# w_out's last halves and the first query group, one token tile after the other, in the layers of the second block

## The chip, the core and the metric

The program runs on one core of a Trainium2 chip. The metric is the device time in microseconds (us) of one execution. PE is TensorE, DVE is VectorE, ACT is ScalarE, POOL is GpSimd, and SP is SyncE, which only issues transfers here.

## The reference

x is 256 tokens of 1024 features. A first block (attention mixer and convolutional FFN) is followed by two layers of a second block; the change lies in these layers.

```python
def rms_norm_2(x, g):
    xf = x.astype(jnp.float32)
    y = xf * lax.rsqrt(jnp.mean(xf * xf, axis=-1, keepdims=True) + EPS)
    return (y * g.astype(jnp.float32)).astype(x.dtype)
...
    merged = gates[:, :, 0] * (oa @ w_branch_na) + gates[:, :, 1] * (ob @ w_branch_swa)
    return merged @ w_out
...
        q = (xc @ w_query).reshape(PEER_CHUNK, PEER_HEADS, 2, half)
        s = jnp.einsum('thpk,pnk->thpn', q, sub_keys).astype(jnp.float32)
        sv, si = lax.top_k(s, PEER_TOPK)
...
        top_s, sel = lax.top_k(cand, PEER_TOPK)
        eidx = jnp.take_along_axis(cidx, sel, axis=-1)
        g = jax.nn.softmax(top_s, axis=-1)
        u = expert_down[eidx]
        vv = expert_up[eidx]
        act = jax.nn.gelu(jnp.einsum('td,thkd->thk', xc, u).astype(jnp.float32), approximate=False)
        return jnp.einsum('thk,thkd->td', (g * act).astype(x.dtype), vv)
...
        x = x + token_mixer(rms_norm_2(x, norm_mix[l]), ...)
        x = x + peer_ffn(rms_norm_2(x, norm_ffn[l]), ...)
```

Each token has 8 heads, and for each head 16 experts are picked out of 16384 by two lists of 128 keys. An expert has a down and an up row of 1024 numbers each. The next layer starts from x when all experts of this one are added.

## The kernel before

**Tiles and exactness.** The 256 tokens are two tiles of 128. Each product with a weight is done in three passes (`product`): weights and features are split into a high part, rounded by ACT (`split_hi`, L517), and a low part, the difference, made by DVE (`split_lo`, L530). `w_lo` counts low parts, `half_done` counts halves that PE has used up.

**Weights.** All weights form one stream of halves of 512 KB, two for a group of 256 output columns. Three slots `W` hold raw halves, `WH` and `WL` hold their parts. Within a layer, halves 42 to 49 are w_out, and 50 to 65 are the query projection, of eight groups. In w_out the order is `WO_ORDER`: groups 0 and 1 take their halves in turn (42 to 45), then group 2 (46, 47) and group 3 (48, 49). SP issues the loads in stream order; half n can be loaded into its slot when the low part of half n-3 is made. Nine query halves (57 to 65) are loaded ahead into places of their own, `HELD`: held half e is issued just behind the load of half 44+e. The last, e = 8, lies over the gains of the norm, so SP first waits until DVE has used those of all column groups (L1059, as `n_peer.hn`). Halves 53 to 56 stand behind it in SP's order.

**End of the mixer.** `wo_pe` (L905) does each half for both tiles. After a group DVE adds the result to `x` (L1965) and multiplies by the gain into `h_norm` (L1972; the norm's factor is applied later). PE turns two chunks of `h_norm` with four transposes (`turned_pe`, L895), ACT copies them as high part (L1609), DVE makes the low part (L1954). Of the first query group PE takes chunks as they become ready, with the weights as the stationary operand (`first_part`), then scores tile 0 against both lists of keys (L1282).

**From scores to gathers.** DVE finds the 8 best of each list (L2069, L2070). The sum of the two best is the first expert: its row goes to POOL at once (L2113), the other seven of the first eight after some 15 more small instructions (L2103). POOL gathers 128 rows of 8 KB with one indirect transfer (L1098) into one of eight ring slots, 512 times in all: 16 for each head and tile. A slot comes free when DVE has made its dot product (L2143, L2166), ACT has made a diagonal matrix of the weight, and PE has added its up rows (L1315). Each later gather into a slot waits for this. ACT's squares of `x` (L1649), whose sum gives the norm, wrote into `Y`, where slots 4 and 5 of the ring lie; the other seven rows therefore waited for them.

The order on every engine is the order in which the code issues, as written by hand.

## Time and profile before

| | us |
|---|---|
| median of 3 runs | 2240.69 (2240.04 to 2241.07) |
| profiled execution, its own time | 2241.91 |
| its span | 2240.1 |
| PE busy | 1990.3 (89%) |
| DVE busy | 1609.4 (72%) |
| ACT busy | 1144.5 (51%) |
| POOL busy | 874.5 (39%) |
| gathers' queue, share of 16 DMA engines' span | 57.8% (536.90 MB) |
| SP's and ACT's queue | 22.4% (157.63 MB) |

Busy shares are means over stages with different limits. The gathers run from 734.6 to 2232 us with a break between the layers. Below, times are from the span's start.

### The profile page before, as it was taken

How to read it: one execution, taken by the hardware profiler on the slowest of the kernel's cores; microseconds unless marked ns; L12 is line 12 of the kernel's file. 1: busy time of each engine (PE TensorE's matmuls, PEld its weight loads, DVE VectorE, ACT ScalarE, POOL GpSimd, SP SyncE). 2: the span in 40 equal slices, each digit the busy share in tenths (PEclk: the TensorE clock that was granted, in tenths of full speed). 3: DMA queues.
4: the chain of work that ended last, by engine and by line, in shares of the span. 5: the costliest groups of instructions: out<-in, count | busy, mean ns of one | idle time of the engine just before them, and what ended most of it. 6: DMA issues, size and time to landing. Idle time of an engine off the chain costs nothing.

```text
span 2240.1 us, 29611 instructions
## 1 busy us (share of the span) xinstructions
PE 1990.3 (89%) x9760; PEld 1302.1 (58%) x9798; DVE 1609.4 (72%) x3230; ACT 1144.5 (51%) x2534; POOL 874.5 (39%) x557
## 2 busy tenths in 40 slices
PE   9999999999999898977777788999899887778877
PEld 8999899998889644422222223889644432222222
DVE  4566777777787877776777765787887776777774
ACT  4455555545554655454454545565655444444443
POOL 0120000000230355566667663040355566666664
PEclk9999999999999999999999999999999999999999
DMA  7544465665636999999999997736899999999998
GB/s 247 172 132 142 148 184 180 185 189 157 219 119 219 381 421 421 421 421 421 421 418 422 420 421 302 233 116 222 334 421 421 421 421 421 422 422 411 422 421 338
DMA packets 120772, 707.23 MB, mean 316 GB/s; under 512 B 13664, under 2 KB 13920, under 8 KB 55008
## 3 DMA queue, kind: packets, MB, share of 16 engines
q0 software_dynamic: 73728, 536.90, 57.8%
q1 hardware_dynamic: 43488, 157.63, 22.4%
q10 hardware_dynamic: 3456, 11.40, 1.5%
q8 instruction: 57, 0.93, 0.2%
q14 instruction: 43, 0.35, 0.0%
HBM read 704.84 MB, written 1.05 MB: 315 GB/s over the span
## 4 chain that ended last, share of the span: by engine, by line
PE 41%; DMA 25%; POOL 11%; DVE 9%; issue 8%; ACT 6%; POOLq 0%; SPq 0%; DVEq 0%; ACTq 0%
DMA work<-in_experts,expert_idx 24%; PE ps L548 11%; POOL work L1098 10%; PE ps L549 10%; PE ps L550 10%; PE ps L1315 6%; DVE work L2166 2%; DVE weights_lo L533 2%; PE ps L687 1%; ACT L1616 1%; ACT L1667 1%; DMA weights<-in_wstream 1%; ACT arena L1672 1%; DVE work L2143 1%; PE ps L713 1%
## 5 line engine op out<-in xcount | busy, mean ns | idle before, releaser
L1315 PE MATMUL ps<-work,arena 128*128 128x512 f32 x2040 | 989.9, 617 | 216.1 <-ACT arena L1672 212.4
L1098 POOL DMA_INDIRECT work<-in_experts,expert_idx x512 | 790.2, 1543 | 621.2 <-PE ps L1315 291.3
L1315 PEld LDWEIGHTS ps<-work,arena 128*128 128x128 f32 x2040 | 359.0, 191 | 821.0 <-ACT arena L1672 516.2
L2166 DVE CUSTOM_DVE_ANT_0 work<-h_norm,work 128x1024 f32<-128x1024 f32 x480 | 588.1, 1225 | 334.5 <-DMA work<-in_experts,expert_idx 320.2
L1667 ACT ACTIVATE small<-small 128x1 f32<-128x1 f32 x512 | 150.2, 293 | 609.1 <-DVE small L2166 588.0
L533 DVE TENSOR_TENSOR weights_lo<-weights,weights_hi 128x1024 fp32r<-128x1024 f32 x280 | 349.8, 1255 | 152.8 <-ACT weights_hi L528 152.1
L548 PE MATMUL ps<-feat_hi,weights_hi 128*128 128x256 f32 x1528 | 445.3, 291 | 7.6 <-DVE weights_lo L533 5.8
L528 ACT ACTIVATE weights_hi<-weights 128x1024 fp32r<-128x1024 f32 x280 | 295.0, 1056 | 286.0 <-PE ps L550 232.6
L549 PE MATMUL ps<-feat_lo,weights_hi 128*128 128x256 f32 x1528 | 432.8, 283 | 0.0
L550 PE MATMUL ps<-feat_hi,weights_lo 128*128 128x256 f32 x1528 | 432.7, 283 | 0.0
L548 PEld LDWEIGHTS ps<-feat_hi,weights_hi 128*128 128x128 f32 x1528 | 293.3, 192 | 18.1 <-issue 9.3
L549 PEld LDWEIGHTS ps<-feat_lo,weights_hi 128*128 128x128 f32 x1528 | 293.6, 192 | 5.4 <-issue 4.8
L550 PEld LDWEIGHTS ps<-feat_hi,weights_lo 128*128 128x128 f32 x1528 | 293.5, 192 | 0.0
L1087 POOL TENSOR_TENSOR work<-arena,consts 128x640 f32<-128x640 f32 x8 | 13.9, 1769 | 525.3 <-issue 445.8
L1672 ACT ACTIVATE arena<-consts,small 128x128 f32<-128x128 f32 x512 | 205.5, 401 | 16.7
L1669 ACT ACTIVATE small<-small,expert_gate 128x1 f32<-128x1 f32 x512 | 150.7, 294 | 16.7
L754 POOL TENSOR_TENSOR work<-work,small 128x1024 f32<-128x1024 f32 (+2 forms) x26 | 60.0, 2310 | 197.3 <-DVE small L744 197.3
L548 PE MATMUL ps<-weights_hi,feat_hi 128*128 128x256 f32 (+2 forms) x416 | 131.4, 316 | 1.8 <-DVE feat_lo L465 0.9
L549 PE MATMUL ps<-weights_lo,feat_hi 128*128 128x256 f32 (+2 forms) x416 | 128.2, 308 | 0.0
L550 PE MATMUL ps<-weights_hi,feat_lo 128*128 128x256 f32 (+2 forms) x416 | 128.2, 308 | 0.0
L1786 DVE SCALAR_TENSOR_TENSOR work<-ps,params,work 128x254 f32<-128x254 f32 (+1 forms) x128 | 55.8, 477 | 51.8 <-ACT work L1469 47.6
L548 PEld LDWEIGHTS ps<-weights_hi,feat_hi 128*128 128x128 f32 x416 | 79.6, 191 | 7.1 <-DVE weights_lo L533 1.5
(250 smaller groups left out, 1912.1 us busy)
## 6 DMA issues: line engine op xcount, KB each, us to landing
weights<-in_wstream SPq DMA_DIRECT2D x280, 512.0 KB, 4.2
work<-in_experts,expert_idx POOLq DMA_INDIRECT x512
arena<-in_wstream SPq DMA_DIRECT2D x12, 512.0 KB, 6.0
arena<-in_na_bias ACTq DMA_DIRECT2D x6, 512.0 KB, 5.3
params<-in_wstream SPq DMA_DIRECT2D x6, 512.0 KB, 5.9
arena<-in_bias ACTq DMA_DIRECT2D x5, 512.0 KB, 4.6
params<-in_par ACTq DMA_DIRECT2D x2, 576.0 KB, 5.3
params<-in_par ACTq DMA_DIRECT2D x1, 1024.0 KB, 6.7
```

Source lines behind the costliest of these rows:

```text
L528: nc.scalar.activation(WH[:, n % SLOTS, :], raw(n), ACT.Copy).then_inc(w_hi, 1)
L533: nc.vector.tensor_tensor(WL[:, n % SLOTS, :], raw(n), WH[:, n % SLOTS, :], ALU.subtract).then_inc(w_lo, 1)
L548: nc.tensor.matmul(out, stat[0], mov[0], start=start, stop=False)
L549: nc.tensor.matmul(out, stat[0], mov[1], start=False, stop=False)
L550: return nc.tensor.matmul(out, stat[1], mov[0], start=False, stop=stop)
L754: nc.gpsimd.tensor_tensor(part, part, view(rsum[b.turn][:, r0:r1], [1, r1 - r0], [0, b.width]), ALU.mult).then_inc(A.probs, 1)
L1098: nc.gpsimd.indirect_dma_start(ring[:, r, :], None, experts, bass.IndirectOffsetOnAxis(ap=EIDX[:, b, c * RING + r:c * RING + r + 1], axis= ...
L1315: ins = nc.tensor.matmul(bank(2 * t + h), DIAG[:, r, :], ring[:, r, D + h * 512:D + (h + 1) * 512], start=False, stop=False)
L1667: nc.scalar.activation(ga[:, r:r + 1], hd[:, r:r + 1], ACT.Gelu, scale=rstd[:, t:t + 1]).then_inc(gelu_ready, 1)
L1669: nc.scalar.activation(gw8[:, r:r + 1], ga[:, r:r + 1], ACT.Copy, scale=GWT[:, b, c * RING + r:c * RING + r + 1]).then_inc(w_ready, 1)
L1672: nc.scalar.activation(DIAG[:, r, :], ident, ACT.Copy, scale=gw8[:, r:r + 1]).then_inc(diag_ready, 1)
L2166: nc.vector.tensor_tensor_reduce(ring[:, r, 0:D], HN[:, t, :], ring[:, r, 0:D], 1.0, 0.0, ALU.mult, ALU.add, hd[:, r:r + 1]).then_inc(dots ...
```

## The change

w_out's halves 46 to 49 are first used for tile 0 alone, then for tile 1; only half 46 for tile 1 stands between them. The first query group is done tile by tile, with the features as stationary operand (its weights are packed so), for tile 0 after half 46's second use, and for tile 1 after all of w_out. Its result then has tokens on the partitions, so PE turns it back (`query0_turned`) between two copies by ACT. Because halves 46 to 48 stay in use longer, their parts lie in room that the ring of gathers takes later (`SPARE`), so the splits of 49 to 51 wait for a half six places back, not three. The adds to `x` and the gains are split by tile for groups 2 and 3. `h_norm` is now counted in six turns, and SP's wait before held half 8 is for the sixth, group 3 of tile 1. The squares go to `arena` and the wait for them is moved behind the index of the seven rows. Held 7 still waits for groups 0 and 1. Tile 1's keys of the first head move behind query group 1.

```diff
+        with nc.sbuf_tensor("work_rounded", [P, 16392], F32R) as work_rounded:
+            SPARE = [work_rounded[:, a:a + 2 * HW] for a in (0, 8200, 14344)]
...
+        def spare(n):
+            local = (n - L_HALF) % L_HALVES - 2 * LG_WO - 4
+            return local if n >= L_HALF and 0 <= local < SLOTS else None
+        def behind_spare(n):
+            return n >= L_HALF and SLOTS <= (n - L_HALF) % L_HALVES - 2 * LG_WO - 4 < 2 * SLOTS
+        def high(n):
+            return WH[:, n % SLOTS, :] if spare(n) is None else SPARE[spare(n)][:, 0:HW]
+        def low(n):
+            return WL[:, n % SLOTS, :] if spare(n) is None else SPARE[spare(n)][:, HW:2 * HW]
...
-            if n >= SLOTS:
-                act.wait_ge(half_done, base + n - SLOTS + 1)
-            nc.scalar.activation(WH[:, n % SLOTS, :], raw(n), ACT.Copy).then_inc(w_hi, 1)
+            if n >= SLOTS and spare(n) is None:
+                act.wait_ge(half_done, base + n - (2 * SLOTS if behind_spare(n) else SLOTS) + 1)
+            nc.scalar.activation(high(n), raw(n), ACT.Copy).then_inc(w_hi, 1)
...
+        HN_TURNS, HI_TURNS = WO + 2, 7
+        def hn_turn(g, t=TT - 1):
+            return (1, 2, 3 + 2 * t, 4 + 2 * t)[g]
+        def turned_pe(pe, nm, l, g, tiles=range(TT)):
+            pe.wait_ge(nm.hn, HN_TURNS * l + hn_turn(g, tiles[0]))
             for c in (2 * g, 2 * g + 1):
-                for t in range(TT):
+                for t in tiles:
                     ins = nc.tensor.transpose(ps[:, c * S + t * P:c * S + (t + 1) * P], HN[:, t, c * P:(c + 1) * P], ident)
...
+        def wo_tile(pe, n, t, b, at, chunks=range(HC)):
+            h = WO_ORDER[n][1]
+            w = split_pe(pe, L_HALF + 2 * LG_WO + n, at)
+            for i in chunks:
+                c = h * HC + i
+                ins = product(ps[:, b * 512 + t * GC:b * 512 + (t + 1) * GC], kept(c, t * P, P), cols(w, i * GC, GC), c == 0, c == KC - 1)
+            return ins
...
-                        sp.wait_ge(n_peer.hn, 4 * l + -(-min(gains_end, D) // GC))
+                        sp.wait_ge(n_peer.hn, HN_TURNS * l + hn_turn(-(-min(gains_end, D) // GC) - 1))
...
-                wo_pe(pe, (lproj_taken, l * N2 + L_PROJ + L_GATE), G_LAYER + LG_WO, l, at, turned=n_peer)
+                taken0 = WO + (WO + 1) * l
+                for n in range(4):
+                    wo_both(pe, (lproj_taken, l * N2 + L_PROJ + L_GATE), G_LAYER + LG_WO, n, l * BR + BR, at)
+                pe.wait_ge(wo_taken, taken0 + 1)
+                wo_tile(pe, 4, 0, 6, at)
+                turned_pe(pe, n_peer, l, 0)
+                wo_tile(pe, 5, 0, 6, at).then_inc(tile0_done, 1)
+                turned_pe(pe, n_peer, l, 1)
+                wo_tile(pe, 6, 0, 5, at).then_inc(tile0_done, 1)
+                turned_pe(pe, n_peer, l, 2, (0,))
+                wo_tile(pe, 7, 0, 5, at).then_inc(tile0_done, 1)
+                wo_tile(pe, 4, 1, 6, at).then_inc(half_done, 1)
+                turned_pe(pe, n_peer, l, 3, (0,))
...
+                def query0(t, b):
+                    for c in range(KC):
+                        if c % HC == 0:
+                            w = split_pe(pe, L_HALF + 2 * LG_PQ + c // HC, at)
+                        if c % 2 == 0:
+                            pe.wait_ge(n_peer.hT, HI_TURNS * l + (1 if c == 0 else c // 2 + 1 + 3 * t))
+                        ins = product(ps[:, b * 512:b * 512 + GC], feat(c, t * P, P), cols(w, c % HC * GC, GC), c == 0, c == KC - 1)
+                        if t and c % HC == HC - 1:
+                            ins.then_inc(half_done, 1)
                     return ins
+                def query0_turned(t, step):
+                    pe.wait_ge(first_query, step)
+                    for part in range(2):
+                        ins = nc.tensor.transpose(ps[:, 5 * 512 + S + part * P:5 * 512 + S + (part + 1) * P], pqT[:, 4 + t, part * P:(part + 1) * P], ident)
+                    ins.then_inc(tile0_done, 1)
...
-                pe.wait_ge(n_peer.hT, l * 4 + 2)
-                parts = [split_pe(pe, L_HALF + 2 * LG_PQ, at)]
-                first_part(0, range(HC))
-                turned_pe(pe, n_peer, l, 3)
-                parts.append(split_pe(pe, L_HALF + 2 * LG_PQ + 1, at))
-                first_part(1, range(HC))
-                pe.wait_ge(n_peer.hT, l * 4 + 3)
-                for part in range(2):
-                    first_part(part, range(4, 6))
-                pe.wait_ge(n_peer.hT, l * 4 + 4)
-                for part in range(2):
-                    first_part(part, range(6, 8)).then_inc(half_done, 1)
-                pe.wait_ge(first_query, l + 1)
+                query0(0, 7).then_inc(tile0_done, 1)
+                wo_tile(pe, 5, 1, 6, at, range(2))
+                query0_turned(0, l * 3 + 1)
+                wo_tile(pe, 5, 1, 6, at, range(2, HC)).then_inc(half_done, 1)
+                pe.wait_ge(first_query, l * 3 + 2)
                 key_score(4, 0, 0, 0).then_inc(first_scored, 1)
-                pe.wait_ge(lproj_taken, l * N2 + L_PROJ + L_GATE + 1)
                 key_score(5, 0, 0, 1).then_inc(first_scored, 1)
-                for part in range(2):
-                    ins = key_score(3, part, 1, part)
-                ins.then_inc(sc_done, 1)
+                wo_tile(pe, 6, 1, 7, at).then_inc(half_done, 1)
+                wo_tile(pe, 7, 1, 7, at).then_inc(half_done, 1)
+                turned_pe(pe, n_peer, l, 2, (1,))
+                turned_pe(pe, n_peer, l, 3, (1,))
+                query0(1, 6)
+                query0_turned(1, l * 3 + 3)
...
+                turned_act(0, 1, (0, TT))
+                act.wait_ge(tile0_done, l * 6 + 2)
+                turned_act(1, 2, (0, 1))
+                act.wait_ge(tile0_done, l * 6 + 3)
+                turned_act(2, 3, (0, 1))
+                turned_act(3, 4, (0, 1))
+                query0_act(0)
+                query0_turned_act(0)
+                act.wait_ge(half_done, wo_halves + 7)
+                turned_act(1, 2, (1, TT))
+                act.wait_ge(half_done, wo_halves + 8)
+                turned_act(2, 5, (1, TT))
                 split_hi(act, L_HALF + 2 * LG_PQ + 2, at)
+                turned_act(3, 6, (1, TT))
...
+                query0_act(1)
                 hi_query(SLOTS)
+                query0_turned_act(1)
+                act.wait_ge(x_ready, l * 3 + 2 * TT + 1)
+                for t in range(TT):
+                    ins = nc.scalar.activation((DIAG.rearrange("p r n -> p (r n)") if t else SC[:, 1:5, :, :].rearrange("p a s n -> p (a s n)")), X[:, t, :], ACT.Square, accum_out=ssq[:, t:t + 1])
+                ins.then_inc(n_peer.sq, 1)
+                hi_query(SLOTS + 1)
+                act.wait_ge(n_peer.var, l + 1)
+                nc.scalar.activation(std, ssq, ACT.Sqrt).then_inc(n_peer.std, 1)
...
+                for n in range(SLOTS, SLOTS + 3):
+                    half_lo(n)
+                added(0, 6, (0, TT), (half_done, wo_halves + wo_done(0)), 1)
+                half_lo(6)
+                half_lo(7)
+                added(1, 7, (0, TT), (half_done, wo_halves + wo_done(1)), 2)
+                half_lo(8)
+                lower(0, 1, (0, TT))
+                added(2, 6, (0, 1), (tile0_done, l * 6 + 1), 3)
+                half_lo(9)
+                lower(1, 2, (0, 1))
+                added(3, 5, (0, 1), (tile0_done, l * 6 + 3), 4)
+                lower(2, 3, (0, 1))
+                lower(3, 4, (0, 1))
...
+                added(2, 6, (1, TT), (half_done, wo_halves + 6), 5)
+                added(3, 7, (1, TT), (half_done, wo_halves + 8), 6)
                 rc.link(nc.vector.tensor_tensor(cand[:, 0:HALF * HALF].rearrange("p (a b) -> p a b", a=HALF), view(sv[:, 0, :], [1, HALF], [0, HALF]),
                                                 view(sv[:, 1, :], [0, HALF], [1, HALF]), ALU.add))
                 rc.link(nc.vector.max(topv[:, 0:HALF], cand[:, 0:HALF * HALF]))
                 rc.link(nc.vector.max_index(sel[:, 0, 0:HALF], topv[:, 0:HALF], cand[:, 0:HALF * HALF]))
-                pick_rows(0, HALF, 3, 1, (n_peer.sq, l + 1)).then_inc(first_rows, 1)
+                lower(1, 5, (1, TT))
+                lower(2, 6, (1, TT))
+                pick_rows(0, HALF, 3, 1).then_inc(first_rows, 1)
+                lower(3, 7, (1, TT))
+                lo_query(2)
                 lo_query(SLOTS)
+                dve.wait_ge(n_peer.sq, l + 1)
```

DVE at the end of w_out, before. `h_norm<-x,params` is the gain of a column group; `weights_lo` is a low part.

```order
L533 TENSOR_TENSOR weights_lo<-weights,weights_hi 128x1024 [waits w_hi] x2
L1965 TENSOR_TENSOR x<-x,ps 128x2x256 [waits half_done]
L1972 TENSOR_TENSOR h_norm<-x,params 128x2x256 [waits wo_taken]
L533 TENSOR_TENSOR weights_lo<-weights,weights_hi 128x1024 [waits w_hi] x2
L1965 TENSOR_TENSOR x<-x,ps 128x2x256 [waits half_done]
L1972 TENSOR_TENSOR h_norm<-x,params 128x2x256 [waits wo_taken]
L1954 TENSOR_TENSOR feat_lo<-ps,feat_hi 128x512 [waits n_peer_hi] x2
L533 TENSOR_TENSOR weights_lo<-weights,weights_hi 128x1024 [waits w_hi]
L1965 TENSOR_TENSOR x<-x,ps 128x2x256 [waits half_done]
L1972 TENSOR_TENSOR h_norm<-x,params 128x2x256 [waits x_ready]
L1954 TENSOR_TENSOR feat_lo<-ps,feat_hi 128x512 [waits n_peer_hi] x2
L533 TENSOR_TENSOR weights_lo<-weights,weights_hi 128x1024 [waits w_hi]
```

DVE at the same place, now; `128x256` and `128x2x128` are pieces for one tile.

```order
L561 TENSOR_TENSOR weights_lo<-weights,weights_hi 128x1024 [waits w_hi]
L2061 TENSOR_TENSOR x<-x,ps 128x2x256 [waits half_done]
L2063 TENSOR_TENSOR h_norm<-x,params 128x2x256 [waits wo_taken]
L561 TENSOR_TENSOR weights_lo<-weights,weights_hi 128x1024 [waits w_hi]
L2048 TENSOR_TENSOR feat_lo<-ps,feat_hi 128x512 [waits n_peer_hi]
L2061 TENSOR_TENSOR x<-x,ps 128x256 [waits tile0_done]
L2063 TENSOR_TENSOR h_norm<-x,params 128x256 [waits wo_taken]
L561 TENSOR_TENSOR weights_lo<-weights,weights_hi 128x1024 [waits w_hi]
L2048 TENSOR_TENSOR feat_lo<-ps,feat_hi 128x2x128 [waits n_peer_hi]
L2061 TENSOR_TENSOR x<-x,ps 128x256 [waits tile0_done]
L2063 TENSOR_TENSOR h_norm<-x,params 128x256 [waits wo_taken]
L2048 TENSOR_TENSOR feat_lo<-ps,feat_hi 128x2x128 [waits n_peer_hi] x2
```

The gain of group 1, second of the first piece, now stands behind one more low part (half 49); groups 2 and 3 come first for tile 0.

ACT at the end of w_out and in the first query group, before. `feat_hi<-ps` copies turned groups; `arena<-ps 128x256` takes a query.

```order
L528 ACTIVATE weights_hi<-weights 128x1024 [waits half_done,w_landed2]
L528 ACTIVATE weights_hi<-weights 128x1024 [waits half_done,w_landed0]
L1609 ACTIVATE feat_hi<-ps 128x512 [waits n_peer_transposed,half_done]
L1609 ACTIVATE feat_hi<-ps 128x512 [waits n_peer_transposed]
L528 ACTIVATE weights_hi<-weights 128x1024 [waits half_done,w_landed1]
L1609 ACTIVATE feat_hi<-ps 128x512 [waits n_peer_transposed,half_done]
L1609 ACTIVATE feat_hi<-ps 128x512 [waits n_peer_transposed]
L528 ACTIVATE weights_hi<-weights 128x1024 [waits half_done,w_landed2]
L1639 ACTIVATE arena<-ps 128x256 [waits half_done] x2
L528 ACTIVATE weights_hi<-weights 128x1024 [waits half_done,w_landed0]
L1645 ACTIVATE arena<-ps 128x256 [waits sc_done]
```

ACT at the same place, now.

```order
L556 ACTIVATE weights_hi<-weights 128x1024 [waits half_done,w_landed2]
L556 ACTIVATE weights_hi<-weights 128x1024 [waits half_done,w_landed0]
L556 ACTIVATE weights_hi<-weights 128x1024 [waits half_done,w_landed1]
L1685 ACTIVATE feat_hi<-ps 128x512 [waits n_peer_transposed]
L1685 ACTIVATE feat_hi<-ps 128x2x128 [waits n_peer_transposed,tile0_done] x2
L1685 ACTIVATE feat_hi<-ps 128x2x128 [waits n_peer_transposed]
L1690 ACTIVATE arena<-ps 128x256 [waits tile0_done]
L1695 ACTIVATE arena<-ps 128x2x128 [waits tile0_done]
L1685 ACTIVATE feat_hi<-ps 128x2x128 [waits n_peer_transposed,half_done] x2
L556 ACTIVATE weights_hi<-weights 128x1024 [waits half_done,w_landed2]
L1685 ACTIVATE feat_hi<-ps 128x2x128 [waits n_peer_transposed]
```

The splits of halves 49, 50 and 51 now stand together ahead of the first copy of turned features; the copies of query and turned query follow, and the split of half 52 comes after w_out's last half.

## Rows read from the trace of the kernel before

**Rows 1.** Windows, layer 0: length, busy time by engine, PEclk, DMA share, GB/s.
```profile
704.00:720.80 16.80, 16.77 (x138) 16.45 (x138) 11.26 (x13) 7.17 (x8) 0.00 (x0) 1.00 0.94 346
720.80:727.00 6.20, 5.64 (x46) 5.44 (x47) 4.93 (x7) 2.63 (x4) 0.00 (x0) 1.00 0.04 15
727.00:733.40 6.40, 6.17 (x52) 5.98 (x52) 3.50 (x10) 3.64 (x6) 0.00 (x0) 1.00 0.92 321
733.40:736.00 2.60, 2.17 (x19) 1.97 (x17) 2.33 (x15) 1.74 (x2) 1.11 (x1) 1.00 0.05 22
736.00:738.75 2.75, 0.00 (x0) 0.00 (x0) 1.27 (x4) 1.39 (x4) 0.26 (x1) 1.00 0.88 265
738.75:742.50 3.75, 3.64 (x19) 3.64 (x20) 3.34 (x16) 1.15 (x2) 3.14 (x3) 0.58 0.96 321
...
785.00:800.00 15.00, 14.92 (x59) 8.48 (x58) 11.98 (x31) 8.49 (x22) 9.70 (x8) 1.00 1.01 418
```

**Rows 2.** The same windows in layer 1.
```profile
1569.60:1575.80 6.20, 5.86 (x49) 5.54 (x48) 4.83 (x7) 2.71 (x5) 0.00 (x0) 1.00 0.04 13
1575.80:1582.00 6.20, 5.97 (x51) 5.78 (x50) 3.40 (x10) 3.56 (x6) 0.00 (x0) 1.00 0.91 336
1582.00:1584.50 2.50, 2.27 (x19) 2.07 (x18) 2.23 (x14) 2.43 (x4) 0.98 (x1) 1.00 0.02 8
```

**Rows 3.** Timeline of POOL: start, length, instruction, idle time before and what ended it.
```profile
734.59 1.11 POOL L1098 DMA_INDIRECT work<-in_experts,expert_idx  x1 [68.74 <-DVE expert_idx L2113]
738.50 1.12 POOL L1098 DMA_INDIRECT work<-in_experts,expert_idx  x1 [2.79 <-DVE expert_idx L2103]
...
754.13 1.34 POOL L1098 DMA_INDIRECT work<-in_experts,expert_idx  x1 [5.03 <-PE ps L1315]
...
774.87 1.03 POOL L1098 DMA_INDIRECT work<-in_experts,expert_idx  x1 [2.38 <-DVE expert_idx L2046]
```

**Rows 4.** Timeline of DVE, from h_norm's second group to the second index.
```profile
714.51 0.69 DVE L1972 TENSOR_TENSOR h_norm<-x,params 128x512 f32<-128x512 f32 x1
715.63 1.23 DVE L533 TENSOR_TENSOR weights_lo<-weights,weights_hi 128x1024 fp32r<-128x1024 f32 x1 [0.43 <-ACT weights_hi L528]
725.58 0.69 DVE L1972 TENSOR_TENSOR h_norm<-x,params 128x512 f32<-128x512 f32 x1
733.48 0.16 DVE L2113 SCALAR_TENSOR_TENSOR expert_idx<-arena 128x1 uint32<-128x1 f32 x1
737.50 0.17 DVE L2103 SCALAR_TENSOR_TENSOR expert_idx<-arena 128x7 uint32<-128x7 f32 x1 [1.48 <-ACT work L1649]
737.59 1.22 DVE L533 TENSOR_TENSOR weights_lo<-weights,weights_hi 128x1024 fp32r<-128x1024 f32 x1
```

**Rows 5.** Timeline of SP's queue: when loads were issued.
```profile
713.90 0.33 SPq L1039 DMA_DIRECT2D weights<-in_wstream  x1
715.23 0.33 SPq L1060 DMA_DIRECT2D params<-in_wstream  x1
716.88 0.33 SPq L1039 DMA_DIRECT2D weights<-in_wstream  x1
726.30 0.33 SPq L1060 DMA_DIRECT2D params<-in_wstream  x1
726.67 0.43 SPq L1039 DMA_DIRECT2D weights<-in_wstream  x1
```

**Rows 6.** Timeline of ACT: high parts of halves 47 to 50.
```profile
708.06 1.06 ACT L528 ACTIVATE weights_hi<-weights 128x1024 fp32r<-128x1024 f32 x1 [1.82 <-DMA weights<-in_wstream]
711.56 1.06 ACT L528 ACTIVATE weights_hi<-weights 128x1024 fp32r<-128x1024 f32 x1 [2.43 <-DMA weights<-in_wstream]
714.54 1.06 ACT L528 ACTIVATE weights_hi<-weights 128x1024 fp32r<-128x1024 f32 x1 [0.41 <-DMA weights<-in_wstream]
717.60 1.06 ACT L528 ACTIVATE weights_hi<-weights 128x1024 fp32r<-128x1024 f32 x1 [2.00 <-DMA weights<-in_wstream]
```

**Rows 7.** Timeline of DVE: the first dot product, and the first that waited for DMA.
```profile
745.84 1.22 DVE L2143 CUSTOM_DVE_ANT_0 work<-h_norm,work 128x1024 f32<-128x1024 f32 x1
784.83 1.23 DVE L2166 CUSTOM_DVE_ANT_0 work<-h_norm,work 128x1024 f32<-128x1024 f32 x1 [0.23 <-DMA work<-in_experts,expert_idx]
```

**Rows 8.** Timeline of PE: half 46's start, spacing, the keys, and half 53.
```profile
710.72 0.47 PE L548 MATMUL ps<-weights_hi,ff_gated_hi 128*128 128x256 f32 x1
717.86 0.28 PE L549 MATMUL ps<-weights_lo,ff_gated_hi 128*128 128x256 f32 x1
717.98 0.28 PE L550 MATMUL ps<-weights_hi,ff_gated_lo 128*128 128x256 f32 x1
731.13 0.41 PE L1282 MATMUL ps<-params,arena 128*128 128x128 f32 x2
738.86 0.39 PE L548 MATMUL ps<-feat_hi,weights_hi 128*128 128x256 f32 x1 [3.29 <-DVE weights_lo L533]
```

128 lines of the change are left out of this document (58 added, 70 removed).

## The prediction

> **What bounds the kernel now.** The page first: PE, VectorE and the DMA engines all look busy, so shares over the whole span decide nothing. Its DMA line shows two long plateaus at 421 GB/s, one per layer of the second block: the 512 expert gathers of 1.05 MB. A later window between 785 and 800 us still has DMA share 1.01 [rows 1], and from 784.83 the dot products wait for the gathers [rows 7]. So once a layer's gathers run, its length is bytes over 421 GB/s, and a change ahead of them is worth exactly what it does to idle DMA time and to the bytes still to be moved when they begin.
>
> Next the windows around the change, layer 0 [rows 1]. Until 720.8 DMA is nearly full (0.94, 346 GB/s). It is idle to 727.0 (share 0.04), busy to 733.4 (0.92, 321 GB/s, 2.05 MB: four weight halves of 0.52 MB), idle to 736.0, and practically full from 736.0 on. Idle in 720.8 to 742.5, window by window: 5.95 + 0.5 + 2.45 + 0.35 + 0.15 = 9.4 us. Layer 1 has the same picture: 6.2 us idle, four halves, 2.5 us idle [rows 2].
>
> The timelines name the events. The first gather is issued at 734.59, 0.95 us after its index; gathers 1 to 7 from 738.50, after the index of 737.50 [rows 3, 4]. Gather 8 waits for slot 0 until 754.13 [rows 3]. SP issues loads in strict order: 51 (w_out has halves 42 to 49, the query 50 on) at 713.90, held half 7 at 715.23, half 52 at 716.88, then held half 8 at 726.30 and half 53 at 726.67, 54 just behind [rows 5]. Held 8 waits for the last `h_norm` column group, written 725.58 to 726.27 [rows 4]; 53 to 55 stand behind it. These four are the 2.05 MB that now fill otherwise idle DMA time.
>
> ScalarE's first splits of halves 47 to 50, at 708.06, 711.56, 714.54 and 717.60, each end a wait on DMA [rows 6]. The weight stream, not PE, sets the pace of w_out's end.
>
> **What the change does, step by step.** No byte and no matmul column is added. PE's w_out products are the same, 0.12 us start to start [rows 8], so 12 of them (a half for one tile) are 1.44 us and 24 are 2.88.
>
> 1. The start. VectorE splits half 47 before it adds column group 0 (`x` waits behind it). Half 47's high part is ready at 708.06 + 1.06, its low part 1.2 later, so the add ends near 711.2 and PE's half 46 starts at 711.3 instead of 710.72 [rows 6, 8]: 0.6 us lost.
> 2. Group 1. PE runs half 46 and 47 for tile 0 and the first turn, 3.3 us, to 714.6. The second turn wants `h_norm` group 1. That add stood at 714.51 before; now it stands behind the low part of half 49. The high part of 49 starts at 714.54 after DMA and a table load [rows 6], the low part ends 716.85, the add and gain (0.7 us each, rows 4) end 718.2. PE waits 3.5 us. I take nothing off for earlier loads: the loads in front are the same and DMA is full.
> 3. ScalarE now splits halves 50 and 51 before it copies the first turned group. 51 lands near 719 (DMA ends all eleven loads queued by then at 720.8), so the copy is done at 720.8, the low part at 721.5, x group 2 and its gain at 722.4. PE: half 48 to 720.1, half 49 for tile 0 from 722.6, half 46 for tile 1 to 725.5.
> 4. Query of tile 0: from 725.7, 2.88 us, to 728.6. Copy (0.38), transposes (0.25), copy, with 0.13 us between engines: keys at 730.2. Before, keys began at 731.13 and the index ended 733.64 [rows 4, 8]: 2.5 us. So index 0 at 732.7 and gather 0 issued at 733.7, 0.9 us earlier.
> 5. Clock. Before, PE waited 3.29 us until 738.86 and then ran with granted clock 0.58 over 738.75 to 742.5, that is mostly at 1.2 GHz [rows 1, 8]. Step 2 makes a wait of the same length in front of half 48. From nothing to some 1.6 us (what the slow stretch of 3.75 us at 0.58 lost); I take 1.0. This eats the 0.9 of step 4: gather 0 starts as before, within 1.
> By the Trainium skill (TensorE: Matmul & The Clock Gate, Part 1) an idle stretch sends TensorE to 1.2 GHz and sustained work brings it back. If that holds here, step 4's gain is gone; without it the sum is 1 us a layer better.
> 6. Tile 1 follows: keys 0.8, halves 48 and 49 for tile 1, 2.88. `h_norm`'s last part, 725.6 to 726.3 before, is ready only at 734.9 to 735.9. Held 8, 53, 54 then are issued 9 us later, and 55 follows the low part of 52, which now stands behind eight more VectorE instructions. Before, they ran while DMA was idle; now they run beside gathers: 2.1 MB at 421 GB/s, 5.0 us that the gathers lose. If other loads' 346 GB/s applied, 6.1.
> 7. The second index loses its wait on ScalarE's squares (1.48 us, rows 4) but stands behind tile 1's adds: 734.9 plus 3.2 of its own and the lows is 738.1, against 737.67. The extra small VectorE instructions (two adds and gains split by tile, about 1 us) are in this.
> 8. Holes in 736.0 to 742.5, 0.5 us, are filled: minus 0.5. The splits in ring room add no work; gather 0 into that room starts after half 46's last product anyway.
> 9. Consumers. Low 53 starts near 742.6 against 737.59, since 53 lands late; the squares, variance and second halves of the keys follow: the first dot product near 753 against 745.84 [rows 4, 7]. Gather 8 would be issued near 758.8 (754.13 before, rows 3). DMA by then holds eight gathers (20 us) and six loads (8 us) from 736: work until about 764, so it does not run dry there. Gathers 12 to 16 are closer: gather 16 (774.87 before) shifts by 7, the queue by 4.5. I charge 0.5, with 0 and 3.5 as ends.
>
> Sum for a layer: 0 + 5.0 - 0.5 + 0.5 = 5.0 us. Two layers: 10. Own time of the profiled execution 2241.91 (span 2240.1), so 2251.9; the median of the runs is 1.2 lower: 2250.7, say 2251. Its own range, 3.5 to 7.5 a layer, is 2248 to 2256.
>
> **Rivals.**
> Ring runs dry. DVE was behind the gathers until 784.83 [rows 7] and so the 7 us of step 9 count in full from gather 12 on: DMA idles 3 us more in each layer, 8 in all, 2256.7. For it: gathers 8 to 15 were paced by slots before. Against: the longer backlog.
> The Trainium skill (DMA: Bandwidth & Descriptors, Queues, rings and completion order) has each DMA engine take turns between queues by packets. Then 53 and 54 land up to twice as late as alone, which feeds this rival; the rows here show both kinds of load in one full stretch but not their shares.
>
> Faster: tile order works as drawn. If weights 49 to 51 are there in time, PE has from 711.3 only work: 5 x 1.44 + 1.3 + 2.88 = 11.4 us to 722.7, index 0 at 726.7, gather 0's data from 729.2 (736.1 before), the last `h_norm` at 729. Then 6.9 earlier, 5.0 for the four halves, 0.5 for holes: 2.4 us less a layer, 2236. It decides if the wait for `h_norm` group 1 stays under 0.5 us. Against: four DMA waits in a row on exactly these halves.
>
> Middle: waits shrink by half, gather 0 starts 3 us earlier, the loads still collide: +2 a layer, 2245.
>
> That nothing happens at all is excluded: both orders differ on the bounding path. Only layer 1's slightly earlier weights speak for the middle.
>
> **How the numbers follow.** Forecast 0.56, dry ring 0.20, middle 0.12, faster 0.12. The likeliest gives 2251. The range takes in the dry ring with a us to spare, 2258, and goes down to 2242, leaving the faster case and little else out. About 0.2% (4.5 us) is what a measurement of this kernel tells from no change. Slower: forecast, dry ring and a third of the middle, 0.80; same: the rest of the middle, 0.08; faster 0.12.
>
> **What would show it.** DMA idle from about 722 to 735 in one piece; held 8 issued at 734 to 736 on SP; gather 0 within 1.5 us of 734.6 and gather 1 near 739; a PE wait of 3 us on `h_norm` before the second turn, and granted clock 0.5 behind it; first dot product 6 to 8 us later; dot 16 about 5 later. Wrong: gather 0 before 731, or held 8 before 731, or a DMA gap between 760 and 790 above 2 us (then the dry ring).

## The result, and the profile after

The changed kernel takes 2256.95 us (median of 4, 2255.06 to 2260.83) against 2240.36 for the kernel before on the same chip: 1.0076 of its time, 95% interval 1.0059 to 1.0094, that is 16.6 us, or 8.3 a layer. The profiled execution is the longest of the four (own time 2260.83, span 2259.0), 3.9 us above the median, so the shifts read below are a little larger than the typical ones.

Windows of the kernel after, layer 0 and then one of layer 1 (columns as in [rows 1]):

```profile
720.80:727.00 6.20, 5.38 (x26) 5.08 (x25) 4.03 (x8) 0.96 (x3) 0.00 (x0) 0.50 0.22 87
727.00:733.40 6.40, 6.40 (x56) 6.40 (x56) 0.86 (x4) 1.15 (x3) 0.00 (x0) 0.99 0.00 0
733.40:736.00 2.60, 2.60 (x24) 2.52 (x22) 2.21 (x11) 0.38 (x1) 0.09 (x1) 1.00 0.00 0
736.00:742.50 6.50, 4.62 (x33) 3.77 (x32) 5.25 (x20) 1.99 (x4) 2.48 (x2) 1.00 0.74 260
755.00:770.00 15.00, 13.91 (x79) 10.22 (x79) 13.65 (x43) 10.38 (x23) 2.28 (x2) 1.00 0.98 378
770.00:785.00 15.00, 13.98 (x50) 7.56 (x50) 14.69 (x38) 11.78 (x27) 6.14 (x6) 1.00 0.95 357
785.00:800.00 15.00, 15.00 (x53) 8.18 (x52) 14.32 (x41) 8.25 (x23) 7.73 (x8) 1.00 1.01 422
...
1620.00:1640.00 20.00, 17.89 (x65) 9.57 (x64) 19.55 (x50) 15.15 (x36) 7.84 (x8) 1.00 0.89 315
```

The same windows of the kernel before that are not among the rows of before:

```profile
755.00:770.00 15.00, 13.97 (x57) 8.03 (x56) 14.62 (x41) 11.11 (x27) 5.73 (x7) 1.00 1.01 422
770.00:785.00 15.00, 13.96 (x51) 7.64 (x50) 14.37 (x39) 10.13 (x27) 6.75 (x7) 1.00 1.01 422
...
1620.00:1640.00 20.00, 19.47 (x69) 10.86 (x70) 18.02 (x52) 10.58 (x31) 9.62 (x10) 1.00 1.01 419
```

Between 727 and 736 DMA moves nothing, where four weight halves ran before [rows 1]. That was forecast. What was not is the second gap: at 755 to 770 and 770 to 785, deep in the gathers, the share is 0.98 and 0.95 and the rate 378 and 357 GB/s against 422. In bytes (rate times length): over 720.8 to 742.5 the kernel before moved 4.14 MB [rows 1] and this one 2.23, 1.91 MB or 4.5 us at 421 GB/s; over 755 to 785 it is (422 - 378) x 15 + (422 - 357) x 15 = 1.64 MB, or 3.9 us. The two make 8.4 us. Gather 255 of this execution is 7.8 us late; the median's 8.3 a layer is close too, but these two stretches are a choice. Over 704 to 800 as a whole it is 355 against 315 GB/s, 3.8 MB or 9.1 us (0.4 MB of it before 720.8), so the bytes give the size to within about 1.5 us and no better. Layer 1 has the second gap as well: 315 against 419 GB/s in 1620 to 1640, 2.1 MB or 4.9 us.

POOL, the gathers 0, 1, 8 and 16 (answers to [rows 3]):

```profile
735.91 1.11 POOL L1151 DMA_INDIRECT work<-in_experts,expert_idx  x1 [70.10 <-DVE expert_idx L2215]
740.92 1.45 POOL L1151 DMA_INDIRECT work<-in_experts,expert_idx  x1 [3.90 <-DVE expert_idx L2205]
...
764.59 1.34 POOL L1151 DMA_INDIRECT work<-in_experts,expert_idx  x1 [14.77 <-PE ps L1391]
...
785.32 1.03 POOL L1151 DMA_INDIRECT work<-in_experts,expert_idx  x1 [2.37 <-DVE expert_idx L2150]
```

Gather 0 is 1.3 us later, gather 1 2.4, but gather 8 and 16 are 10.5 us later. Gather 8 waits for PE to empty slot 0.

VectorE: `h_norm` group 1, both indices, the low parts of halves 53 and 55, the first dot product (answers to [rows 4, 7]):

```profile
717.31 0.69 DVE L2063 TENSOR_TENSOR h_norm<-x,params 128x512 f32<-128x512 f32 x1
...
734.79 0.16 DVE L2215 SCALAR_TENSOR_TENSOR expert_idx<-arena 128x1 uint32<-128x1 f32 x1
...
739.93 0.17 DVE L2205 SCALAR_TENSOR_TENSOR expert_idx<-arena 128x7 uint32<-128x7 f32 x1
...
746.44 1.23 DVE L561 TENSOR_TENSOR weights_lo<-weights,weights_hi 128x1024 fp32r<-128x1024 f32 x1 [4.88 <-ACT weights_hi L556]
...
754.20 1.23 DVE L561 TENSOR_TENSOR weights_lo<-weights,weights_hi 128x1024 fp32r<-128x1024 f32 x1 [0.59 <-ACT weights_hi L556]
...
756.46 1.22 DVE L2252 CUSTOM_DVE_ANT_0 work<-h_norm,work 128x1024 f32<-128x1024 f32 x1
```

SyncE's queue (answers to [rows 5]): held 7, held 8, and halves 53 on.

```profile
718.03 0.33 SPq L1113 DMA_DIRECT2D params<-in_wstream  x1
...
736.87 0.33 SPq L1113 DMA_DIRECT2D params<-in_wstream  x1
737.24 15.39 SPq L1092 DMA_DIRECT2D weights<-in_wstream  x5
```

ScalarE: the high part of 53, the copy of head 0's scores (L1746), the high part of 55:

```profile
745.35 1.06 ACT L556 ACTIVATE weights_hi<-weights 128x1024 fp32r<-128x1024 f32 x1 [3.47 <-DMA weights<-in_wstream]
...
752.77 0.38 ACT L1746 ACTIVATE arena<-ps 128x256 f32<-128x256 f32 x1 [2.98 <-PE ps L1360]
753.05 1.05 ACT L556 ACTIVATE weights_hi<-weights 128x1024 fp32r<-128x1024 f32 x1
```

PE: the second turn, half 53's first product, the scores of head 1, the first ring slot (answers to [rows 8]):

```profile
718.06 1.12 PE L942 MATMUL ps<-consts,h_norm 128*128 128x128 f32 x4 [3.70 <-DVE h_norm L2063]
...
747.72 0.58 PE L576 MATMUL ps<-feat_hi,weights_hi 128*128 128x256 f32 x1 [2.48 <-DVE weights_lo L561]
...
754.73 0.46 PE L1329 MATMUL ps<-params,arena 128*128 128x128 f32 x2 [2.00 <-ACT arena L1727]
...
761.90 3.60 PE L1391 MATMUL ps<-work,arena 128*128 128x512 f32 x8
```

The same two in the kernel before, the high part of half 53 on ScalarE and the first ring product on PE:

```profile
731.61 1.05 ACT L528 ACTIVATE weights_hi<-weights 128x1024 fp32r<-128x1024 f32 x1
...
751.44 3.60 PE L1315 MATMUL ps<-work,arena 128*128 128x512 f32 x8
```

These rows name two things that hold the consumers: half 53, issued 10.6 us later and landing 8.1 us after its issue (737.24 to 745.35; before, it was issued at 726.67 and ScalarE split it at 731.61, 4.9 us later, without a wait for DMA), and the scores' copy, which ScalarE began only after 2.98 us of waiting for PE, with half 55's high part, its low part and the first dot product behind it. The experiments had to say which of them counts.

The Trainium skill (DMA: Bandwidth & Descriptors, Queues, rings and completion order) has the engines take turns between queues by packets. The trace fits this and does not prove it: held half 8, the first load of its burst both times, took 3.5 us from issue to landing before and 7.2 here, beside gather 0; the queues' shares were not read. Gathers are not the only way to a long landing: half 54 of the kernel before, third in its burst (issued at 727.15), took 7.1 us with no gather under way.

### The profile page after: what moved, and what is told of

Same layout as the page of the kernel before. It is cut to its first block, busy times and chain, and to the rows that moved or that the text cites. A ratio compares the mean times of both kernels' runs of the same rounds, so it can differ in the third digit from the quotient of the medians.

```text
span 2259.0 us, 29653 instructions
## 1 busy us (share of the span) xinstructions
PE 2003.5 (89%) x9768; PEld 1312.4 (58%) x9802; DVE 1610.5 (71%) x3244; ACT 1146.5 (51%) x2544; POOL 872.1 (39%) x557
## 4 chain that ended last, share of the span: by engine, by line
PE 39%; DMA 26%; POOL 11%; DVE 10%; issue 8%; ACT 6%; POOLq 0%; DVEq 0%; SPq 0%; ACTq 0%
DMA work<-in_experts,expert_idx 24%; POOL work L1151 10%; PE ps L576 10%; PE ps L577 10%; PE ps L578 10%; PE ps L1391 6%; DVE weights_lo L561 2%; DVE work L2275 2%; DMA weights<-in_wstream 2%; PE ps L723 1%; DVE work L2252 1%; ACT L1715 1%; ACT L1761 1%; ACT arena L1766 1%; PE ps L749 1%
## 5 line engine op out<-in xcount | busy, mean ns | idle before, releaser
L561 DVE TENSOR_TENSOR weights_lo<-weights,weights_hi 128x1024 fp32r<-128x1024 f32 x274 | 342.5, 1255 | 154.5 <-ACT weights_hi L556 154.1
L576 PE MATMUL ps<-feat_hi,weights_hi 128*128 128x256 f32 x1496 | 436.5, 292 | 5.5 <-DVE weights_lo L561 3.7
L556 ACT ACTIVATE weights_hi<-weights 128x1024 fp32r<-128x1024 f32 x274 | 288.6, 1056 | 282.4 <-PE ps L578 228.2
L577 PE MATMUL ps<-feat_lo,weights_hi 128*128 128x256 f32 x1496 | 424.0, 283 | 0.0
L578 PE MATMUL ps<-feat_hi,weights_lo 128*128 128x256 f32 x1496 | 423.8, 283 | 0.0
L576 PEld LDWEIGHTS ps<-feat_hi,weights_hi 128*128 128x128 f32 x1496 | 287.6, 192 | 16.0 <-issue 9.3
L577 PEld LDWEIGHTS ps<-feat_lo,weights_hi 128*128 128x128 f32 x1496 | 287.7, 192 | 5.3 <-issue 4.8
L578 PEld LDWEIGHTS ps<-feat_hi,weights_lo 128*128 128x128 f32 x1496 | 287.5, 192 | 0.0
```

Source lines behind the costliest of these rows:

```text
L556: nc.scalar.activation(high(n), raw(n), ACT.Copy).then_inc(w_hi, 1)
L561: nc.vector.tensor_tensor(low(n), raw(n), high(n), ALU.subtract).then_inc(w_lo, 1)
L576: nc.tensor.matmul(out, stat[0], mov[0], start=start, stop=False)
L577: nc.tensor.matmul(out, stat[0], mov[1], start=False, stop=False)
L578: return nc.tensor.matmul(out, stat[1], mov[0], start=False, stop=stop)
```

## The experiments

All times are medians beside runs of the kernel before on the same chip (2240.36 to 2241.09 over the calls). "First slot" is the start of the first ring product on PE in layer 0, read like the row at 761.90 above, and "g8", "g255" are the issue of gathers 8 and 255, each minus that of the kernel before (751.44, 754.13 and 1370.97). The shifts carry what lies ahead of the change too: SyncE issues one and the same load at 703.92 before, and between 703.71 (e5) and 705.09 (e12) in the others, so shifts of up to a us mean little.

| kernel | us | ratio (95%) | first slot | g8 | g255 |
|---|---|---|---|---|---|
| after | 2256.95 | 1.0076 (1.0059 to 1.0094) | +10.5 | +10.5 | +7.8 |
| e1_loads_first | 2261.03 | 1.0088 (1.0072 to 1.0105) | +11.0 | +11.0 | +8.6 |
| e2_gains_first | 2252.03 | 1.0042 (1.0026 to 1.0059) | +11.5 | +11.5 | +9.6 |
| e3_both | 2253.25 | 1.0053 (1.0036 to 1.0070) | +8.2 | +8.2 | +5.7 |
| e4_squares_alone | 2240.67 | 0.9998 (0.9988 to 1.0007) | -1.4 | -1.4 | -0.8 |
| e5_before_late_loads | 2263.08 | 1.0103 (1.0086 to 1.0120) | +11.5 | +11.6 | +9.4 |
| e6_kept_warm | 2255.94 | 1.0067 (1.0050 to 1.0084) | +10.8 | +10.8 | +8.7 |
| e8_keys_first | 2247.05 | 1.0025 (1.0015 to 1.0034) | +3.5 | +3.6 | +1.8 |
| e9_keys_and_adds | 2240.44 | 1.0000 (0.9990 to 1.0010) | 0.0 | +0.1 | -2.4 |
| e11_consumers_first | 2239.87 | 1.0000 (0.9991 to 1.0009) | +3.9 | +3.9 | +0.5 |
| e12_before_exp_first | 2240.52 | 0.9997 (0.9988 to 1.0006) | +0.3 | +0.3 | -0.4 |
| e13_after_keys_first | 2257.00 | 1.0066 (1.0053 to 1.0080) | +10.7 | +10.8 | +8.5 |
| e14_slot_before_55 | 2243.01 | 1.0011 (1.0002 to 1.0020) | +1.5 | +1.5 | +0.6 |

**e1_loads_first: the loads back in the idle stretch.** In the kernel after, held half 8 is issued behind half 54, so that 53 and 54 don't wait for `h_norm`:

```diff
+                e = {8: -1, 10: 8}.get(e, e)
```

> The changed kernel with one edit on SP: held query half 8 is issued behind half 54 instead of behind half 52, so halves 53 and 54 no longer stand behind a wait for the last h_norm group (736.87 in the changed kernel) and are issued near 718.8 and 723.6, in time in which DMA is idle. Theory A (the loads behind held half 8 come 10 us late, the split of half 53 at 745.35 and with it squares, norm and the first dot product at 756.46 wait for them, and the ring runs dry): first dot product near 752, gather 8 near 760 instead of 764.59, 4 to 6 us less in a layer, 2245 to 2249 us. Rival B (what costs is the start of w_out's end: the gain of group 1 behind half 49's split, a PE wait of 3.7 us and the slow clock behind it; the loads are hidden anyway): under 1 us a layer, 2255 to 2257.

Nothing came back. The loads did move (DMA share 0.24 in 722 to 736, half 53 split at 741.71), but ScalarE and PE then waited elsewhere. ScalarE, the scores' copy and half 55's high part:

```profile
751.35 0.38 ACT L1747 ACTIVATE arena<-ps 128x256 f32<-128x256 f32 x1 [5.21 <-remote]
751.63 1.05 ACT L556 ACTIVATE weights_hi<-weights 128x1024 fp32r<-128x1024 f32 x1
```

PE in the same execution, the scores of head 1:

```profile
753.31 2.05 PE L1330 MATMUL ps<-params,arena 128*128 128x128 f32 x8 [4.81 <-ACT arena L1728]
```

ScalarE waits 5.21 us for head 0's keys for tile 1, which the change put behind query group 1 on PE; `take_query(1)` stands behind that copy in ScalarE's order, and PE waits 4.81 us for it. Not all of the 5.21 us is PE's order. The key products themselves are these:

```profile
747.89 0.60 PE L1361 MATMUL ps<-params,arena 128*128 128x128 f32 x4
```

From their end to the copy there are 2.9 us for which the profile names no cause (`remote`); e3 has the same (products from 745.58, copy at 749.04). This stays open. The other limit was not fully off either: half 55 is issued at 741.51 as in the kernel after. In bytes, 2.5 us came back in 720.8 to 736 (106 GB/s, 1.6 MB against 0.5), and 2.0 us were lost again in 755 to 785 (339 against 367 GB/s): bytes moved early are lost later when slots don't come free.

**e2_gains_first: the column groups ahead of the low parts.** VectorE adds groups 0, 1 and 2 before it splits halves 48 to 51, and ScalarE copies the first turned group before the high parts of 49 and 50:

```diff
-                for n in range(SLOTS, SLOTS + 3):
-                    half_lo(n)
+                half_lo(3)
+                half_lo(4)
                 added(0, 6, (0, TT), (half_done, wo_halves + wo_done(0)), 1)
-                half_lo(6)
-                half_lo(7)
+                half_lo(5)
                 added(1, 7, (0, TT), (half_done, wo_halves + wo_done(1)), 2)
-                half_lo(8)
+                half_lo(6)
+                added(2, 6, (0, 1), (tile0_done, l * 6 + 1), 3)
```

> The changed kernel with the order on VectorE and ScalarE edited: adds and gains of groups 0, 1 and 2 stand ahead of the low parts of halves 47, 48 and 49 on VectorE, the first turned group is copied ahead of the high parts of 49 and 50 on ScalarE, and the second ahead of that of 51. SP's order is the changed kernel's. PE should have no wait of 3.7 us and no slow clock; index 0 near 728 to 730 instead of 734.95, the last h_norm group 5 us earlier, and so the loads behind held half 8 too. Theory A: the loads are still collided with gathers but come 5 us earlier, the first dot product near 751: 5 us less a layer, 2244 to 2248. Rival B (the early wait is all of it): back at 2240 or below.

The 3.7 us wait went, but a wait of 3.84 us for group 3 of tile 0 came at 724.37, since the low parts of 50 and 51 now stood ahead of that add. Gather 0 was only 0.7 us later than in the kernel before, and gather 8 still 11.5. The median is 4.9 us under that of the kernel after; the profiled execution was its longest (2258.15), so the table's shifts don't show where these went.

**e3_both.** Both edits:

> Both edits: halves 53 and 54 ahead of held half 8 on SP, and gains ahead of splits on VectorE and ScalarE. If both delays are what the change lost, gather 0 is issued near 729 to 731 (734.59 before), gather 1 near 734, the first dot product near 743 to 746, DMA is idle less than 8 us in all in 720 to 742: 3 to 5 us less a layer than the kernel before, 2231 to 2236. If something else costs (the products by tile, tile 1's work in front of query groups 1 and 2 on PE), 2240 to 2246.

Far off: 2253.25. The first dot product came at 752.73, and ScalarE again waited 5.22 us for the keys. This, with e1, turned the theory from "late bytes" to "late consumers": the gathers 0 and 1 stand where they stood before (-1.1 and 0.0 us), half 53 is there, and yet the first slot is 8.2 us late and the time 12 us longer.

**e4_squares_alone: one part of the change in the kernel before.** ScalarE's squares are written elsewhere, and the index of rows 1 to 7 does not wait for them:

```diff
-                pick_rows(0, HALF, 3, 1, (n_peer.sq, l + 1)).then_inc(first_rows, 1)
+                pick_rows(0, HALF, 3, 1).then_inc(first_rows, 1)
                 lo_query(SLOTS)
+                dve.wait_ge(n_peer.sq, l + 1)
```

> The kernel before with one part of the change alone: the squares of x are written outside the ring's room, and the index of rows 1 to 7 no longer waits for them. That index ends near 736.1 instead of 737.67. Theory A (DMA practically full from 736.0 on, so an earlier gather 1 fills only holes of 0.5 us): 0 to 0.5 us less a layer, 2239.5 to 2240.5. Rival C (each us of the second index is a us of the layer): 1.5 a layer, 2237.4.

No difference, within 0.12%.

**e5_before_late_loads: the other way round.** e4, and held half 8 waits until the index of rows 1 to 7 is written; no engine's order is touched:

```diff
+                    if e == 8:
+                        sp.wait_ge(first_rows, l * 2 + 2)
```

> The kernel before (with the squares written elsewhere and the index of rows 1 to 7 not waiting for them, which alone measured 0.9998 of before) and one more wait on SyncE: held half 8, and with it halves 53 to 55 behind it, is issued only when the index of rows 1 to 7 is written, near 737 us instead of 726.3. PE, VectorE and ScalarE keep the order of before. Theory A (late loads are what the change costs: 2.1 MB moved from idle DMA time to beside the gathers, 5.0 us a layer): 2250 to 2252, first dot product 3 to 6 us late. Theory D (the change costs because PE, ScalarE and VectorE now have the second token tile's work ahead of the first ring slots; loads alone cost little): under 2246. Both together, because late half 53 also delays the first dot product: 2255 or more, with holes in DMA near 770 to 785.

22 us longer, with the late loads alone. PE, half 53's first product:

```profile
746.88 0.58 PE L548 MATMUL ps<-feat_hi,weights_hi 128*128 128x256 f32 x1 [11.76 <-DVE weights_lo L533]
```

ScalarE, its high part:

```profile
744.51 1.06 ACT L528 ACTIVATE weights_hi<-weights 128x1024 fp32r<-128x1024 f32 x1 [13.26 <-DMA weights<-in_wstream]
```

PE stands still for 11.76 us. In 755 to 770 DMA moves 280 GB/s. So late loads (half 53, and 54 and 55 behind it) are by themselves enough for the whole shift of the first slot. In e1 half 53 was early and the first slot as late, with the keys' wait in front of it: the two are in parallel, each hidden behind the other.

**e6_kept_warm: the clock.** The kernel after, with 14 products of zeros in front of the second turn:

```diff
                 wo_tile(pe, 5, 0, 6, at).then_inc(tile0_done, 1)
+                for _ in range(14):
+                    nc.tensor.matmul(bank(4), ZERO[:, 0:P], ZERO[:, :], start=True, stop=True)
                 turned_pe(pe, n_peer, l, 1)
```

> The kernel after with 14 more matmuls on zeros (128x512 bf16, into a free bank) between w_out's half 47 of tile 0 and the turn that waits 3.7 us for h_norm group 1: TensorE is busy in that wait. If the clock after the wait (granted 0.50 in 718 to 726) is worth the 1.0 us a layer of my step 5, and time saved ahead of index 0 counts in full: 2254 to 2255. If nothing hangs on it since the consumers set the pace: 2256 to 2258. If the whole slow stretch of 8 us at half speed counts: 2249 or less. Index 0 then at 733 instead of 734.8.

The window behind the wait, kernel after:

```profile
718.00:728.00 10.00, 9.12 (x45) 8.82 (x46) 5.32 (x10) 2.31 (x4) 0.00 (x0) 0.54 0.32 110
```

And in this one:

```profile
718.00:728.00 10.00, 6.86 (x45) 6.62 (x45) 6.02 (x11) 2.91 (x5) 0.00 (x0) 0.83 0.36 127
```

The granted clock (0.54: most of the stretch at 1.2 of 2.4 GHz, after PE had stood idle for 3.70 us) rose to 0.83 and PE was busy for 6.86 instead of 9.12 us. But the next wait for `h_norm`, at 723.26, grew from 0.82 to 2.38 us, and the index of row 0 came at 734.98 (734.79 after). As this execution began the stretch 0.7 us later than that of the kernel after (the load named above at 704.60 against 703.87), the clock was worth some 0.5 us at the index and at the first slot at most. The times alone would not tell 1 us a layer (2255.94 against 2256.95, with overlapping intervals); the rows do.

**e13_after_keys_first: only the keys moved, in the kernel after.**

```diff
-                    group_fm(pe, G_LAYER + LG_PQ + j, pq_bank(j), at)
+                    half_fm(pe, G_LAYER * 2 + 2 * (LG_PQ + j), pq_bank(j), 0, at)
                     if j == 1:
                         ...
                             ins = key_score(3, part, 1, part)
                         ins.then_inc(sc_done, 1)
+                    half_fm(pe, G_LAYER * 2 + 2 * (LG_PQ + j) + 1, pq_bank(j), 1, at)
```

> The kernel after with only the keys of head 0, tile 1, moved on PE from behind query group 1 to between its halves. In the kernel after ScalarE's copy of these scores (752.77, after 2.98 us of waiting for PE) stands ahead of half 55's high part, and that ahead of the first dot product at 756.46; half 53's late landing (745.35) is left as it is. Theory D: first dot 1.5 to 3 us earlier, the same for gather 8, so 2250 to 2254. Rival (late halves 53 and 54 pin the consumers, and this wait is only in their shadow): 2256 to 2258.

The rival was right here: the interval overlaps that of the kernel after. ScalarE's high part of half 53:

```profile
746.26 1.06 ACT L556 ACTIVATE weights_hi<-weights 128x1024 fp32r<-128x1024 f32 x1 [3.40 <-issue]
```

PE's first product of it:

```profile
748.63 0.58 PE L576 MATMUL ps<-feat_hi,weights_hi 128*128 128x256 f32 x1 [0.28 <-DVE weights_lo L561]
```

The trace names no releaser for the 3.40 us; half 53 was issued at 738.23 behind held half 8, so it is its landing again. ScalarE's squares stand behind it, and VectorE's second key halves and first dot product (756.86) behind these. The scores' copy did move, from 752.77 to 750.61, and nothing came of it: the keys' wait was in the shadow of half 53.

**e8_keys_first: both limits off.** e3 and the keys' move of e13:

> Experiment e3_both (loads first, column groups' adds first: 2253.25) with one more move: on PE the keys of head 0 for tile 1 stand between the two halves of query group 1 instead of behind both. In e3 ScalarE waited 5.2 us for these keys before its copy of the scores (749.04), and half 55's high part (749.32), half 55's low part on VectorE (750.47) and the first dot product (752.73) stood behind that copy. Theory D (the consumers' late start is the cost): copy at 744, first dot at 747.5 to 748.5 instead of 752.7, PE's first ring slot 4 to 5 us earlier, and the time falls by 3 to 5 us a layer: 2243 to 2247. Rival (bytes and backlog at DMA decide; consumers catch up before the ring is dry): the first dot moves but the time stays at 2252 to 2254.

First dot 749.50, first slot 4.7 us earlier than in e3, and 6.2 us off the time (2253.25 to 2247.05), at the edge of what was expected. The same move was worth nothing in e13 and 6 us here.

**e9_keys_and_adds: tile order as drawn.** The add of group 3 for tile 0 stands ahead of the low parts of halves 50 and 51, and ScalarE's copies of the turned groups ahead of the high part of 51:

```diff
                 added(3, 5, (0, 1), (tile0_done, l * 6 + 3), 4)
+                half_lo(8)
                 lower(2, 3, (0, 1))
                 lower(3, 4, (0, 1))
+                half_lo(9)
```

> e8_keys_first with VectorE and ScalarE mended once more: the add and gain of column group 3 for tile 0 stand ahead of the low parts of halves 50 and 51, and the copies of turned groups 2 and 3 ahead of the high part of 51. In e3 PE waited 3.7 us for that gain (h_norm at 723.5) and index 0 came at 732.40. Theory D with tile order working as drawn: wait gone, index 0 at 728.5 to 730, gather 0 near 730, first dot 745 to 746, and 2236 to 2242. Rival: half 51, landing near 720.5, then its split and the query's second half set index 0, which comes at 731 or later; time as e8_keys_first within 2 us.

POOL, gathers 0, 1 and 8:

```profile
729.35 1.12 POOL L1152 DMA_INDIRECT work<-in_experts,expert_idx  x1 [63.55 <-DVE expert_idx L2221]
734.37 1.46 POOL L1152 DMA_INDIRECT work<-in_experts,expert_idx  x1 [3.90 <-DVE expert_idx L2211]
...
754.19 1.41 POOL L1152 DMA_INDIRECT work<-in_experts,expert_idx  x1 [9.95 <-PE ps L1394]
```

ScalarE's high part of half 56, and PE's first ring slot:

```profile
746.11 1.06 ACT L556 ACTIVATE weights_hi<-weights 128x1024 fp32r<-128x1024 f32 x1 [1.50 <-DMA weights<-in_wstream]
...
751.40 3.70 PE L1394 MATMUL ps<-work,arena 128*128 128x512 f32 x8 [1.28 <-ACT arena L1771]
```

Its windows (columns as in [rows 1]):

```profile
722.00:736.00 14.00, 11.64 (x89) 10.52 (x89) 8.50 (x32) 3.82 (x8) 2.57 (x2) 1.00 0.52 183
755.00:770.00 15.00, 13.91 (x56) 8.07 (x55) 14.62 (x41) 10.99 (x27) 5.76 (x7) 1.00 0.99 398
770.00:785.00 15.00, 13.98 (x51) 7.54 (x49) 14.39 (x40) 10.12 (x27) 6.78 (x7) 1.00 1.00 399
```

The whole 16.6 us are back, and not one more. Gathers 0 and 1 are issued 5.2 and 4.1 us earlier than in the kernel before, but the first dot product stands at 745.82 (745.84 before), gather 8 at 754.19 (754.13), and the earlier start is paid back at 755 to 785, with 398 and 399 GB/s instead of 422. The ring holds eight gathers; a start ahead of the consumers only fills it sooner. What holds the first slot here is no longer PE: it has finished query group 2 by 749.7 and waits 1.28 us for ScalarE's diagonal. The exponential that leads to it stands behind the high part of half 56, for which ScalarE waits 1.50 us on DMA. Half 56 is issued when half 53's low part is made, and took 8.5 us to land. It is the same in e8 and e13 (PE waits 1.14 and 0.81 us for the diagonal, ScalarE 1.36 and 1.02 for the load): a third limit behind the two.

**e11_consumers_first: the consumers forward too.** On top of e9: ScalarE's squares ahead of its copy of query 0, the second key halves ahead of the low part of 53, the low part of 55 behind the first two dot products, the exponential ahead of the second scores' copy:

```diff
+                act.wait_ge(n_peer.rstd, l + 1)
+                gate_exp(0, 0)
                 take_scores(1)
                 hi_query(SLOTS + 3)
-                act.wait_ge(n_peer.rstd, l + 1)
-                gate_exp(0, 0)
```

> e9_keys_and_adds (2240.44; gathers 0 to 7 issued 4 to 5 us before those of the kernel before, first dot product and gather 8 where they were) with the consumers moved forward: ScalarE's squares ahead of its copy of query 0 of tile 1, VectorE's second key halves ahead of the low part of 53, the low part of 55 behind the first two dot products, ScalarE's exponential ahead of the second scores' copy. First dot at 742 to 743 instead of 745.8, index of the second eight rows near 748 to 749 instead of 751.4; PE's first slot stays behind query group 2, at 749.8 instead of 751.4. Theory D (only the consumers' start counts once the gathers begin early enough): gather 8 at 752 to 753 instead of 754.2 and 1.5 to 3 us a layer: 2234.5 to 2237.5. Rival (PE's query groups set it, since no matmul moves): 2239 to 2241.

The first dot came 2.1 us earlier (743.71), but the first slot 3.9 us later. ScalarE, the high part of half 55:

```profile
744.44 1.06 ACT L556 ACTIVATE weights_hi<-weights 128x1024 fp32r<-128x1024 f32 x1 [3.24 <-DMA weights<-in_wstream]
```

PE, the scores of head 1:

```profile
746.65 1.22 PE L1330 MATMUL ps<-params,arena 128*128 128x128 f32 x8 [3.40 <-ACT arena L1732]
```

SyncE's queue, the issue of half 55 and the two behind it:

```profile
736.19 0.33 SPq L1092 DMA_DIRECT2D weights<-in_wstream  x1
```

The low part of 52 moved 1.1 us back, so half 55 was issued at 736.19 instead of 735.04, and landed 8.2 us later instead of 5.6. ScalarE waited for it with `take_query(1)` behind, PE waited 3.40 us, and group 2 began at half clock. The time stayed at 1.0000 (0.9991 to 1.0009): by gather 16 the 3.9 us of the first slot were down to 0.7 (775.55 against 774.87).

**e14_slot_before_55: PE's order once more.** e11, with PE's products of half 55 behind the first slot:

```diff
                             slot(0, l * USES + k * PASSES + c, r)
+                            if (k, c, r) == (0, 0, 0):
+                                half_fm(pe, G_LAYER * 2 + 2 * (LG_PQ + 2) + 1, pq_bank(2), 1, at)
```

> e11_consumers_first with PE's products of half 55 (2.9 us) behind the first ring slot instead of ahead of it: PE's first slot waits then for ScalarE's diagonal alone, near 748 instead of 749.8. Theory D: gather 8 moves to 750 to 751, another 1 to 2 us a layer: 2232 to 2236. Rival (gather 8 then waits for its index, or slot 1 and the second route's keys come later by the same 2.9 us): within 1 us of e11.

The first slot is 2.4 us earlier than in e11, but the time 3.1 us longer. The same 2.9 us of products now stand in front of slot 1; that this is the reason is argued, not shown.

**e12_before_exp_first: the old order with the exponential forward.** e4, the low part of 55 behind the first two dot products, and on ScalarE:

```diff
                 take_scores(1)
-                hi_query(SLOTS + 3)
                 act.wait_ge(n_peer.rstd, l + 1)
                 gate_exp(0, 0)
+                hi_query(SLOTS + 3)
```

> The kernel before in its own order, with the squares written elsewhere and no wait for them ahead of the index (0.9998 alone), and two moves: the low part of half 55 behind the first two dot products on VectorE, and the exponential ahead of the high part of half 56 on ScalarE. Theory D: first dot at 744.5 instead of 745.8, index of the second eight rows and gather 8 about 1.5 to 2.5 us earlier than 754.13, and 1 to 2 us a layer: 2237 to 2239. Rival (PE opens its accumulators at 751.2 behind query group 2 whatever these do): 2240 to 2241.

First dot 744.19 (1.65 us earlier), first slot 751.74, time 0.9997 of before. PE opens its accumulators at 751.30, behind query group 2, as the rival has it.

No version is faster than the kernel before by more than its interval; e9, the change with its order mended, equals it.

## Why the prediction was right in its range and wrong in its middle

The direction and the range (2242 to 2258) hold, but the time, 2256.95, is not that of the likeliest case (2251, own range 2248 to 2256). It is that of the rival with the dry ring, which had 0.20 and 2256.7. Its sign, a DMA gap above 2 us between 760 and 790, came out too (3.9 us). That its number is met to 0.3 us is luck: it had 5 us of loads and 3 us of gap from consumers 7 us late, and the rows have 4.5 and 3.9 from consumers 10.5 us late.

- The reading ahead of the steps, that the weight stream and not PE sets the pace of w_out's end, is one-sided: [rows 1] have PE busy for 16.77 of 16.80 us until 720.8, and in e2, with the adds ahead of the low parts, the wait of 3.70 us went (0.63 us for a low part remained) with the same loads. VectorE's order made that wait.
- Step 1 (half 46 at 711.3): PE began it at 710.86, 0.14 us later than before, not 0.6.
- Step 2 (group 1, wait of 3.5 us to 718.2): 3.70 us, to 718.06.
- Steps 3 and 4 (index 0 at 732.7): 734.79. Of the 2.1 us, 0.82 are a second wait of PE, for `h_norm` group 2 at 722.56; the rest was not taken apart. Gather 0 was 1.3 us later than before, inside the 1.5 that was given.
- Step 5 (clock, 1.0 us): the clock did fall (0.50 in 720.8 to 727), but e6, which took most of that away, moved the index by half a us at most and the time not beyond its interval. This term should have been nearly nothing.
- Step 6 (loads moved beside gathers, 5.0 us): the issue at 734.9 to 735.9 was 736.87. With step 8's 0.5 us off, 4.5 us were forecast and 4.5 are in the bytes. But these are not bytes that can be had back by themselves (e1 returned 2.5 us of them and gained nothing), and the term left out what the loads are for: half 53 is the next thing that PE, VectorE and ScalarE need. e5 shows it: the late loads alone, in the old order, cost 22 us, not 10.
- Step 7 (second index at 738.1): 739.93.
- Step 8 (-0.5) is measured only together with step 6.
- Step 9 (consumers, charged 0.5 with 3.5 as the end) is the step that failed. The first dot was put near 753 and came at 756.46; gather 8 was put near 758.8 and came at 764.59. The working let half 53's low part start at 742.6; it started at 746.44, because the load took 8.1 us behind gathers, and behind it came a slow clock on PE and the scores' copy on ScalarE. It then argued that eight gathers and six loads keep DMA busy to 764. That is roughly what the windows show (1.02 in 742.5 to 755, 0.98 to 770), but gathers 8 to 16 were 10.5 us late, and the gap behind was 3.9 us, above the end given.
- The sum 5.0 - 0.5 + 0.5 reads, with what the windows show, 4.5 + 3.9 = 8.4 a layer: 2241.91 + 16.8 - 1.2 = 2257.5. This is book-keeping after the fact and not two causes, since e1 moved bytes from the one gap to the other and left the total. In the profiled execution gather 255 is 7.8 us late and layer 1 adds 11.2 (gather 511 is +18.9). The first slot of layer 1 is late by 10.8 us more than gather 255, as in layer 0 (10.5); what differs is that layer 0 makes up 2.7 us behind it and layer 1 nothing. In e13, of the same time as the median, gather 511 is +15.1. Why this one execution did not make it up stays open.
- The faster case failed twice over. Its condition (PE's wait for group 1 under 0.5 us) wasn't met; and e9, where the order runs as drawn and gather 0 goes out at 729.35, shows that even then nothing is gained, since gather 8 waits for a slot whose dot product, diagonal and PE products come no earlier than before (754.19 against 754.13). Of 5.2 us at gather 0, nothing reaches gather 8.

So the cause, as shown: the time follows when the consumers give back the ring's slots, and not when the gathers begin. In nine kernels of the table g255 is the first slot's shift less 1.7 to 2.7 us; in e11 it is 3.4 less, in e12 and e14 0.7 and 0.9, and e4 alone goes the other way, by 0.6. Large shifts of the first slot therefore tell the time, small ones don't (e11: +3.9 and no loss, e14: +1.5 and 2 us). That slot was held by two limits in parallel, the late loads from half 53 on (e5 alone: +11.5) and the second tile's work with the keys behind query group 1 (e1: +11.0, with half 55 still late). Removing either alone changes nothing (e1, e13); removing both, with e2's order, leaves 3.5 (e8), and with the adds mended 0 (e9). e1 and e13 together without e2's order was not run, so the share of that order is known only from e2 alone (+11.5) and from e8 to e9.

## What to carry to other kernels

When a transfer is moved from an idle stretch into a busy one, charge its bytes, and then look up who waits for it: its latency there (8.1 us here for half 53, under 5 in the idle stretch) falls on that consumer. A ring that is filled early gains nothing until its first slot is given back, so follow the change to the first release, not to the first issue. When two limits stand in parallel, each experiment that takes one away says "no effect"; take both away before calling either harmless.

## What was not expected of the hardware

- Held half 8 (0.52 MB), the first load of its burst, landed 3.5 us after its issue in an idle stretch and 7.2 us after it beside gather 0. Half 55 landed 5.6 us after its issue in e9 and 8.2 in e11, where it was issued 1.1 us later. But without any gather the third load of a burst took 7.1 us as well (half 54, before).
- In e1 and e3 the signal for the last key products reached ScalarE some 3 us after the profile has them done (748.5 to 751.35, 746.2 to 749.04). No run shows why.
- Fourteen 128x512 bf16 products of zeros in an idle stretch raised the granted clock over 718 to 728 from 0.54 to 0.83, without an effect on the time beyond the interval.
